# The eight new tokens' tile moved to second place in the output projection, its high and low halves in one stationary operand

## The chip, the cores and the metric

The kernel runs on one core of a Trainium2 chip. The metric is the device time of one execution in microseconds; the kernel before has a median of 1685.89 us over three runs.

## What is computed

One layer of a decoder for 1024 prompt tokens and 8 new tokens (`x_sample`), D = 1024. The part that matters comes after the two branches have been mixed:

```python
mix = jax.nn.sigmoid(ga) * y_conv + jax.nn.sigmoid(gb) * y_attn
x = x + mix @ w_o
x = x + hier_moe(rms_norm(x, norm2_g), w_rg, b_rg, w_re, b_re, w_gate, w_up, w_down)
```

`hier_moe` picks for each token one of 4 groups and two of its 8 experts (32 experts in all), and adds their weighted outputs. All products are taken in full fp32 accuracy.

## The kernel before

The 1032 tokens lie in nine tiles: tiles 0 to 7 have 128 prompt tokens each, tile 8 has the 8 new tokens. A product of two fp32 matrices is made from three products of fp32r parts, hi x hi, hi x lo and lo x hi, where lo is the rest that hi leaves.

**The stage of the change** lies between the projections before it (ending at 923.7 us of the trace) and the experts' stage (from 1070.8 us). On TensorE `step_d(n)`, n = 0 to 8, multiplies tile n of `mix` with `w_o`. The tile's `mix_hi` or `mix_lo`, 128 x up to 128, is the stationary operand, and `wo_hi` or `wo_lo`, 128 x 512, moves. For each of the 8 slices k of D there are six matmuls (lines 1019, 1021 and 1023, two output halves each), so 48 for a tile, also for the tile of 8 tokens. Between them, at k = 0, 2, 4 and 5, stand the small products for the tiles before: `rank(n - 2)` (lines 973 and 974, from the picks of tile n - 2), `turn_x2(n - 1)` (line 980, transposes), `route(n - 1)` (line 989, the router's logits) and `enter(n - 2)` (line 995, expert lists). TensorE runs its program in order, and waits where such a product isn't ready for it.

**VectorE** does for each n, in this order: `residual` (line 1827, adds the projection's PSUM to x2, two instructions), `turned` (1832, copies the transposes), `place(n - 1)`, `second_norm` (1836 and 1840, which writes the one buffer `xn` and first waits until the earlier `xn` has been written to memory), `address(n - 1)`, `mix_split(n + 2)` (1803) and `choose` (1855 to 1882, some twenty short instructions, each waiting for the last, of which line 1879 writes the `picks`). ScalarE has the squares, the other half of the copy, the root, and the high part of `mix`.

**GpSimd** writes `xn` to memory for each tile (line 620; after tile 0 also 120 filler rows, line 635), enters tokens into lists in memory by indirect DMA (626), and after the ninth tile waits for all writes of `xn` and for `gidx`, then gathers the rows of experts 0 and 1 (643). **SyncE** loads four weight chunks of 1 MB before and during step 1 (the fourth after `proj_done` 1), writes each x2 to memory (492), loads five more chunks as soon as the ninth projection is done (480), and goes on with the rest only when both gathers have landed (502 and 503). TensorE bridges the wait with `keep_busy`, then `turn_x(0)` (line 1048) needs the first gather.

Of the kernel before, what the change touches and what calls it, by code (L numbers as in the profile page):

```python
# [53 lines left out]
    0, 128, 256, 257, 265, 281, 313, 331, 347, 355, 356, 365, 365, 493)  # L54

# [51 lines left out]
def program(nc, x_prompt, x_sample, cache_conv, cache_k, cache_v, norm1_g, w_in, conv_w, w_conv_out,  # L107
# [11 lines left out]
    with ExitStack() as ctx:  # L119
# [273 lines left out]
        def _(sp):  # L393
# [152 lines left out]
        def _(pool):  # L546
# [75 lines left out]
            def enter_lists(n, rows):  # L622

                pool.wait_ge(adr_done, n + 1)
                for k in range(2):
                    pool.indirect_dma_start(out=list_dram, out_offset=bass.IndirectOffsetOnAxis(ap=adr[0:rows, 2 * n + k:2 * n + k + 1], axis=0),
                                            in_=tok_u[0:rows, 2 * n + k:2 * n + k + 1], in_offset=None,
                                            bounds_check=LISTROWS * NE - 1, oob_is_err=False).then_inc(listed, 16)

            for n in range(NT):  # L630
                if n >= 2:
                    enter_lists(n - 2, P)
                write_xn(n, P if n < 8 else B8)
# [34 lines left out]
            for n in range(NT - 2, NT):  # L668
                enter_lists(n, P if n < 8 else B8)
# [48 lines left out]
        def _(pe):  # L718
# [258 lines left out]
            def turn_x2(n, rows):  # L977
                pe.wait_ge(x2_done, n + 1)
                for k in range(KT):
                    mm = pe.transpose(bank[4 + k // 4][:, P * (k % 4):P * (k % 4) + rows], x2[0:rows, n, P * k:P * k + P], ident[0:rows, 0:rows])  # L980
# [18 lines left out]
            def step_d(n, rows):  # L999
# [1090 lines left out]
```

## Time and profile before

| | us |
|---|---|
| median of 3 runs | 1685.89 |
| lowest, highest | 1684.85, 1685.95 |
| span of the profiled execution | 1682.9 |

The span is 3.0 us under the median. It is that of the trace's first to last record; what lies outside is outside the trace.

| engine | busy us | share |
|---|---|---|
| TensorE matmul | 1613.2 | 96% |
| VectorE | 1104.4 | 66% |
| ScalarE | 845.3 | 50% |
| GpSimd | 231.8 | 14% |

The shares are means over stages with different limits. Of the chain of work that ended last 88% is TensorE and 6% DMA. The stretches and single waits below say more than the shares. In the rows, `[0.66 <-ACT rms L1360]` means that the engine sat idle for 0.66 us before this instruction, until ScalarE's line 1360 released it. A matmul's printed duration includes the overlap with its neighbours; the chain's pieces don't overlap.

### The profile page before, as it was taken

The numbers are of one execution on the slowest core, as the hardware profiler recorded it, in microseconds if no ns is written. First come the engines' busy times: TensorE is split into PE (matmuls) and PEld (weight loads), VectorE is DVE, ScalarE is ACT, GpSimd is POOL, SyncE is SP. The second block draws the span as 40 slices with busy tenths as digits, with TensorE's granted clock in tenths as the row PEclk, the third lists the DMA queues.
The fourth block names the chain that finished last, engine by engine and source line by source line (L and its number), as shares of the span: only waits on it lengthen the run. The fifth ranks groups of instructions, "written<-read, shape, count | busy, mean of one in ns | idle before, by whom it ended". The sixth has DMA issues, their size and how long they took to land.

```text
span 1682.9 us, 26202 instructions
## 1 busy us (share of the span) xinstructions
PE 1613.2 (96%) x9427; PEld 1470.9 (87%) x9427; DVE 1104.4 (66%) x1967; ACT 845.3 (50%) x1234; POOL 231.8 (14%) x245
## 2 busy tenths in 40 slices
PE   5999999999999999999999999799999999999992
PEld 4999999999999999999999887688888888877781
DVE  5332588888887232114214676898998998888893
ACT  6011366666665321112112211678878778778783
POOL 1111011110110000000000111322122122232310
PEclk9999999999999999999999999799999999999996
DMA  5252111111112111131113712999999999999966
GB/s 151 72 137 79 55 51 51 50 49 39 50 50 88 30 39 50 50 137 52 50 50 126 291 71 82 357 393 379 370 377 376 380 375 379 369 373 370 361 222 224
DMA packets 131857, 305.30 MB, mean 181 GB/s; under 512 B 30404, under 2 KB 92080, under 8 KB 106936
## 3 DMA queue, kind: packets, MB, share of 16 engines
q1 hardware_dynamic: 115415, 267.76, 43.3%
q0 software_dynamic: 16384, 36.76, 7.5%
q8 instruction: 37, 0.61, 0.2%
q14 instruction: 21, 0.16, 0.0%
HBM read 282.81 MB, written 40.41 MB: 192 GB/s over the span
## 4 chain that ended last, share of the span: by engine, by line
PE 88%; DMA 6%; DVE 3%; issue 1%; ACT 1%; SPq 0%; DVEq 0%; POOLq 0%; ACTq 0%
PE bank L725 10%; PE bank L727 9%; PE bank L726 9%; PE bank L1071 8%; PE bank L1059 6%; PE bank L1061 6%; PE bank L1060 6%; PE bank L871 5%; PE bank L873 5%; PE bank L872 5%; DMA e_raw<-in_w_e_gate_dram 5%; PE bank L1019 2%; PE bank L1021 2%; PE bank L1023 2%; PE bank L832 2%; PE bank L1048 1%
## 5 line engine op out<-in xcount | busy, mean ns | idle before, releaser
L1967 DVE TENSOR_TENSOR e_lo<-e_raw,e_hi 128x2048 fp32r<-128x2048 f32 x192 | 433.4, 2288 | 55.4 <-ACT e_hi L1378 52.5
L1378 ACT ACTIVATE e_hi<-e_raw 128x2048 fp32r<-128x2048 f32 x192 | 364.5, 1920 | 50.0 <-DMA e_raw<-in_w_e_gate_dram 20.0
L1167 ACT ACTIVATE w_hi<-w_raw 128x1024 fp32r<-128x1024 f32 x68 | 71.6, 1054 | 325.5 <-DMA w_raw<-in_w_in_dram 182.2
L1493 DVE TENSOR_TENSOR w_lo<-w_raw,w_hi 128x1024 fp32r<-128x1024 f32 x68 | 83.2, 1223 | 203.4 <-ACT w_hi L1167 203.4
L1059 PE MATMUL bank<-e_hi,xT_hi 128*128 128x512 f32 x512 | 205.4, 401 | 3.4 <-DVE xT_lo L1978 3.4
L725 PE MATMUL bank<-h_hi,w_hi 128*128 128x344 f32 x624 | 202.5, 324 | 1.1 <-DVE h_lo L1512 1.1
L1061 PE MATMUL bank<-e_hi,xT_lo 128*128 128x512 f32 x512 | 201.5, 394 | 0.0
L1060 PE MATMUL bank<-e_lo,xT_hi 128*128 128x512 f32 x512 | 201.3, 393 | 0.0
L726 PE MATMUL bank<-h_lo,w_hi 128*128 128x344 f32 x624 | 199.6, 320 | 0.0
L727 PE MATMUL bank<-h_hi,w_lo 128*128 128x344 f32 x624 | 199.6, 320 | 0.0
L871 PE MATMUL bank<-h_hi,w_hi 128*128 128x344 f32 x576 | 190.2, 330 | 0.0
L873 PE MATMUL bank<-h_hi,w_lo 128*128 128x344 f32 x576 | 184.2, 320 | 0.0
L872 PE MATMUL bank<-h_lo,w_hi 128*128 128x344 f32 x576 | 184.1, 320 | 0.0
L725 PEld LDWEIGHTS bank<-h_hi,w_hi 128*128 128x128 f32 x624 | 117.8, 189 | 5.0 <-issue 3.5
L1059 PEld LDWEIGHTS bank<-e_hi,xT_hi 128*128 128x128 f32 x512 | 96.2, 188 | 26.6 <-issue 6.2
L727 PEld LDWEIGHTS bank<-h_hi,w_lo 128*128 128x128 f32 x624 | 117.8, 189 | 0.0
L726 PEld LDWEIGHTS bank<-h_lo,w_hi 128*128 128x128 f32 x624 | 117.6, 188 | 0.0
L1061 PEld LDWEIGHTS bank<-e_hi,xT_lo 128*128 128x128 f32 x512 | 96.1, 188 | 22.9
L1060 PEld LDWEIGHTS bank<-e_lo,xT_hi 128*128 128x128 f32 x512 | 96.2, 188 | 20.6
L872 PEld LDWEIGHTS bank<-h_lo,w_hi 128*128 128x128 f32 x576 | 108.7, 189 | 0.0
L871 PEld LDWEIGHTS bank<-h_hi,w_hi 128*128 128x128 f32 x576 | 108.5, 188 | 0.0
L873 PEld LDWEIGHTS bank<-h_hi,w_lo 128*128 128x128 f32 x576 | 108.2, 188 | 0.0
(351 smaller groups left out, 3164.3 us busy)
## 6 DMA issues: line engine op xcount, KB each, us to landing
e_raw<-in_w_e_gate_dram SPq DMA_DIRECT2D x64, 1024.0 KB, 19.9
e_raw<-in_w_e_up_dram SPq DMA_DIRECT2D x64, 1024.0 KB, 21.1
e_raw<-in_w_e_down_dram SPq DMA_DIRECT2D x64, 1024.0 KB, 21.6
w_raw<-in_w_in_dram SPq DMA_DIRECT2D x104, 256.0 KB, 3.3
a_spill<-y_sb POOLq DMA_DIRECT2D x8, 516.0 KB, 4.0
a_raw<-a_spill SPq DMA_DIRECT2D x2, 2064.0 KB, 12.9
x_tok<-in_x_prompt_dram SPq DMA_DIRECT2D x4, 1024.0 KB, 10.7
w_raw<-in_w_attn_out_dram SPq DMA_DIRECT2D x32, 128.0 KB, 3.0
```

The lines of the kernel that those rows point to most:

```text
L725: pe.matmul(out, wh, xh, start=i == 0, stop=False)
L726: pe.matmul(out, wh, xl, start=False, stop=False)
L727: mm = pe.matmul(out, wl, xh, start=False, stop=i == len(pairs) - 1)
L871: pe.matmul(DN[c][:, 0:CH], w_hi[:, (s + 1) % 3, k, :], h_hi[:, k, cols], start=k == 0, stop=False)
L872: pe.matmul(DN[c][:, 0:CH], w_hi[:, (s + 1) % 3, k, :], h_lo[:, k, cols], start=False, stop=False)
L873: mm = pe.matmul(DN[c][:, 0:CH], w_lo[:, (s + 1) % 3, k, :], h_hi[:, k, cols], start=False, stop=k == KT - 1)
L1059: pe.matmul(out, xT_hi[:, par, kk, :], wh, start=kk == 0, stop=False)
L1060: pe.matmul(out, xT_hi[:, par, kk, :], wl, start=False, stop=False)
L1061: mm = pe.matmul(out, xT_lo[:, par, kk, :], wh, start=False, stop=kk == KT - 1)
L1071: mm = pe.matmul(bank[first_bank + x][:, :], a[:, kk, :], w[:, 1024 * k + 512 * x:1024 * k + 512 * x + 512], start=st, stop=kk == 3 and a ...
L1378: A.activation(e_hi[:, slot % 4, :], e_raw[slot][:, :], ACT.Copy).then_inc(e_hi_done, 1)
L1967: V.tensor_tensor(e_lo[slot][:, :], e_raw[slot][:, :], e_hi[:, slot % 4, :].bitcast(F32), ALU.subtract).then_inc(e_lo_done, 1)
```

## The change

The order of the tiles becomes 0, 8, 1, 2, ... 7 (`TILE`). What was indexed by n is indexed by `TILE[n]`, and `ROWS_AT[n]` gives a tile's tokens. For the tile of 8 tokens the high part lies in columns 0 to 7 and the low part in columns 32 to 39 of one stationary operand of 40 columns (columns 8 to 31 are set to zero). One pass over `wo_hi` and one over `wo_lo` give both parts' products, in 32 matmuls; the rows 0 to 7 and 32 to 39 of PSUM are both added to x2 by VectorE, in four instructions for two. The ninth tile is now tile 7, with 128 tokens. The filler rows of the sums come from tile 0.

```diff
+TILE = (0, 8, 1, 2, 3, 4, 5, 6, 7)
+ROWS_AT = tuple(8 if t == 8 else 128 for t in TILE)
...
-            def begin_sums(n, rows):
+            def begin_sums(n):
+                rows, tile = ROWS_AT[n], TILE[n]
                 sp.wait_ge(x2_done, n + 1)
-                sp.dma_start(sum_rows[0:rows, n, :], x2[0:rows, n, :]).then_inc(sums_begun, 16)
+                sp.dma_start(sum_rows[0:rows, tile, :], x2[0:rows, tile, :]).then_inc(sums_begun, 16)
 
             for n in range(8):
-                begin_sums(n, P)
-            sp.dma_start(sum_rows[B8:P, 8, :], x2[B8:P, 7, :]).then_inc(sums_begun, 16)
+                begin_sums(n)
+            sp.dma_start(sum_rows[B8:P, 8, :], x2[B8:P, 0, :]).then_inc(sums_begun, 16)
...
-                    begin_sums(8, B8)
+                    begin_sums(8)
                     for par in range(2):
                         sp.wait_ge(gathered[par], 16)
...
-            def write_xn(n, rows):
+            def write_xn(n):
+                rows, tile = ROWS_AT[n], TILE[n]
                 pool.wait_ge(xn_done, n + 1)
-                pool.dma_start(xn_rows[0:rows, n, :], xn[0:rows, :]).then_inc(xn_written, 16)
...
@@ -1004,17 +1011,22 @@
...
                     if k == 0 and n >= 2:
-                        rank(n - 2, par, P)
+                        rank(n - 2, par, ROWS_AT[n - 2])
                     if k == 2 and n >= 1:
-                        turn_x2(n - 1, P)
+                        turn_x2(n - 1, ROWS_AT[n - 1])
                     if k == 4 and n >= 1:
                         if n == 1:
                             pe.wait_ge(router_loaded, 96)
-                        route(n - 1, P)
+                        route(n - 1, ROWS_AT[n - 1])
...
                     if k == 5 and n >= 2:
-                        enter(n - 2, par, P)
+                        enter(n - 2, par, ROWS_AT[n - 2])
+                    half = [slice(0, 512), slice(512, D)]
+                    if TILE[n] == 8:
+                        for w, last in ((wo_hi, False), (wo_lo, k == KT - 1)):
+                            for x in range(2):
+                                mm = pe.matmul(bank[2 * par + x][0:40, :], mh[:, k, 0:40], w[:, k, half[x]], start=k == 0 and not w is wo_lo, stop=last)
+                        continue
                     out = [bank[2 * par + x][0:rows, :] for x in range(2)]
-                    half = [slice(0, 512), slice(512, D)]
                     for x in range(2):
                         pe.matmul(out[x], mh[:, k, 0:rows], wo_hi[:, k, half[x]], start=k == 0, stop=False)
                     for x in range(2):
...
-                step_d(n, P if n < 8 else B8)
+                step_d(n, ROWS_AT[n])
             rank(7, 1, P)
-            turn_x2(8, B8)
-            route(8, B8)
+            turn_x2(8, P)
+            route(8, P)
             enter(7, 1, P)
-            rank(8, 0, B8)
-            enter(8, 0, B8)
+            rank(8, 0, P)
+            enter(8, 0, P)
...
-                    A.activation(mix_hi[:, n % 2, :, 0:rows], mix[:, :, n * P:n * P + rows], ACT.Copy).then_inc(mix_hi_done, 1)
+                    at0 = TILE[n] * P
+                    A.activation(mix_hi[:, n % 2, :, 0:rows], mix[:, :, at0:at0 + rows], ACT.Copy).then_inc(mix_hi_done, 1)
...
-            mix_split(1, P)
+            mix_split(1, B8)
             for n in range(NT):
-                rows = P if n < 8 else B8
+                rows = ROWS_AT[n]
...
@@ -1800,7 +1813,11 @@
             def mix_split(n, rows):
                 dve.wait_ge(mix_hi_done, n + 1)
                 hi, lo = (mix_hi[:, n % 2, :, 0:rows], mix_lo[:, n % 2, :, 0:rows]) if n else (mix0_hi[:, :, :], mix0_lo[:, :, :])
-                V.tensor_tensor(lo, mix[:, :, n * P:n * P + rows], hi.bitcast(F32), ALU.subtract).then_inc(mix_lo_done, 1)
+                if TILE[n] == 8:
+                    V.memset(mix_hi[:, n % 2, :, B8:32].bitcast(F32), 0.0)
+                    lo = mix_hi[:, n % 2, :, 32:32 + B8]
+                at0 = TILE[n] * P
+                V.tensor_tensor(lo, mix[:, :, at0:at0 + rows], hi.bitcast(F32), ALU.subtract).then_inc(mix_lo_done, 1)
...
             def residual(n, rows):
                 dve.wait_ge(proj_done, n + 1)
-                dve.wait_ge(x_loaded[n // 2], 32)
+                dve.wait_ge(x_loaded[TILE[n] // 2], 32)
+                if TILE[n] == 8:
+                    for x in range(2):
+                        dst = x2[0:rows, 8, 512 * x:512 * x + 512]
+                        ins = V.tensor_tensor(dst, dst, bank[2 * (n % 2) + x][32:32 + rows, :], ALU.add)
+                    step.after(ins)
                 for x in range(2):
-                    dst = x2[0:rows, n, 512 * x:512 * x + 512]
+                    dst = x2[0:rows, TILE[n], 512 * x:512 * x + 512]
                     ins = V.tensor_tensor(dst, dst, bank[2 * (n % 2) + x][0:rows, :], ALU.add)
                 ins.then_inc(x2_done, 1)
...
-            mix_split(1, P)
+                V.tensor_copy(adr[0:r, 2 * TILE[n]:2 * TILE[n] + 2], adr_f[0:r, :]).then_inc(adr_done, 1)
+
+            mix_split(1, B8)
...
-                rows = P if n < 8 else B8
+                rows = ROWS_AT[n]
...
                 if n > 0:
-                    address(n - 1, (n - 1) % 2, P)
+                    address(n - 1, (n - 1) % 2, ROWS_AT[n - 1])
                 if n + 2 < NT:
-                    mix_split(n + 2, P if n + 2 < 8 else B8)
+                    mix_split(n + 2, ROWS_AT[n + 2])
                 choose(n, n % 2, rows)
-            place(8, 0, B8)
...
-            address(8, 0, B8)
+            address(8, 0, P)
```

**TensorE, step 1.** The first rows below are before, from the last of step 0 over step 1's slices k = 0 and 1 and the transposes of tile 0 (line 980) to its slice k = 2; `x_131` is x2, `bank` is PSUM.

```order
L1023 MATMUL bank<-wo_hi,mix_lo 128x512 x2
L1019 MATMUL bank<-wo_hi,mix_hi 128x512 x2
L1021 MATMUL bank<-wo_lo,mix_hi 128x512 x2
L1023 MATMUL bank<-wo_hi,mix_lo 128x512 x2
L980 MATMUL bank<-tab,x_131 128x128 x8
L1019 MATMUL bank<-wo_hi,mix_hi 128x512 x2
L1021 MATMUL bank<-wo_lo,mix_hi 128x512 x2
L1023 MATMUL bank<-wo_hi,mix_lo 128x512 x2
L1019 MATMUL bank<-wo_hi,mix_hi 128x512 x2
```

After, where lines 1027 and 987 are the new tile's matmuls and the transposes:

```order
L1035 MATMUL bank<-wo_hi,mix_lo 128x512 x2
L1027 MATMUL bank<-wo_hi,mix_hi 40x512 x2
L1027 MATMUL bank<-wo_lo,mix_hi 40x512 x2
L1027 MATMUL bank<-wo_hi,mix_hi 40x512 x2
L1027 MATMUL bank<-wo_lo,mix_hi 40x512 x2
L987 MATMUL bank<-tab,x_131 128x128 x8
L1027 MATMUL bank<-wo_hi,mix_hi 40x512 x2
L1027 MATMUL bank<-wo_lo,mix_hi 40x512 x2
```

The transposes of tile 0 now stand behind eight matmuls of step 1 instead of twelve; so do, further on, the router's products, and step 1 ends sixteen matmuls sooner.

**VectorE, behind `choose` of tile 0.** Before:

```order
L1879 TENSOR_TENSOR picks<-hots 128x32 [waits dve_step]
L1882 TENSOR_SCALAR hv<-hots,tab 128x32 x4
L1827 TENSOR_TENSOR x_131<-x_131,bank 128x512 [waits x_loaded0,proj_done]
L1827 TENSOR_TENSOR x_131<-x_131,bank 128x512
L1832 COPY h2T<-bank 128x512 [waits xnT_psum]
```

After (the adds of step 1 are lines 1845 and 1849):

```order
L1901 TENSOR_TENSOR picks<-hots 128x32 [waits dve_step]
L1904 TENSOR_SCALAR hv<-hots,tab 128x32 x4
L1845 TENSOR_TENSOR x_131<-x_131,bank 8x512 [waits x_loaded4,proj_done]
L1845 TENSOR_TENSOR x_131<-x_131,bank 8x512
L1849 TENSOR_TENSOR x_131<-x_131,bank 8x512 [waits dve_step]
L1849 TENSOR_TENSOR x_131<-x_131,bank 8x512
L1854 COPY h2T<-bank 128x4x8 [waits xnT_psum]
```

The step has two adds more, and the second pair waits for the first.

**GpSimd, the last writes and the first gathers.** Before:

```order
L626 DMA token_lists<-tok_u,adr 36864x1 [waits adr_done]
L626 DMA token_lists<-tok_u,adr 36864x1
L620 DMA normed_rows<-xn 8x1024 [waits xn_done]
L643 DMA xg<-normed_rows,gidx 128x1024 [waits gidx_done,sq2_done,xn_written]
L643 DMA xg<-normed_rows,gidx 128x1024
L626 DMA token_lists<-tok_u,adr 36864x1 [waits adr_done]
```

After (lines 626, 650 and 633 are the write, the gather and the lists):

```order
L633 DMA token_lists<-tok_u,adr 36864x1 [waits adr_done]
L633 DMA token_lists<-tok_u,adr 36864x1
L626 DMA normed_rows<-xn 128x1024 [waits xn_done]
L650 DMA xg<-normed_rows,gidx 128x1024 [waits gidx_done,sq2_done,xn_written]
L650 DMA xg<-normed_rows,gidx 128x1024
L633 DMA token_lists<-tok_u,adr 36864x1 [waits adr_done]
```

The last write of `xn`, on which both gathers wait, has 128 rows where it had 8.

## Rows read from the trace of the kernel before

**Rows 1.** Stretches: us, busy us of PE, PEld, DVE, ACT, POOL, PEclk, DMA, GB/s.
```profile
943.50:955.50 12.00, 12.00 (x61) 10.05 (x61) 7.43 (x40) 2.88 (x5) 1.07 (x2) 1.00 1.01 404
1050.00:1064.00 14.00, 5.12 (x45) 3.96 (x43) 10.93 (x65) 6.69 (x9) 1.36 (x2) 0.61 0.91 363
1064.00:1070.00 6.00, 4.84 (x23) 4.72 (x24) 4.23 (x14) 0.60 (x1) 4.78 (x5) 0.50 0.49 163
1450.00:1500.00 50.00, 49.15 (x230) 39.73 (x229) 43.82 (x29) 38.20 (x33) 15.19 (x8) 1.00 1.01 374
```

**Rows 2.** Chain that ended last, steps 1 to 3: start us, us, what.
```profile
941.46 1.71 PE bank L989 x16
...
944.18 0.46 PE bank L1023 x2
...
948.74 0.14 PE bank L973 x2
...
963.26 0.14 PE bank L973 x2
```

**Rows 3.** Timeline, tile 0 beside step 1: start us, us, engine, line, operation.
```profile
939.29 0.46 DVE L1911 TENSOR_TENSOR wr<-wr,cols 128x288 f32<-128x288 f32 x1 [2.85 <-DMA slot_no<-in_table_dram]
...
941.00 0.16 DVE L1836 RECIPROCAL rms<-rms 128x1 f32<-128x1 f32 x1 [0.66 <-ACT rms L1360]
...
947.64 0.19 DVE L1879 TENSOR_TENSOR picks<-hots 128x32 f32<-128x32 f32 x1
...
948.77 1.28 DVE L1827 TENSOR_TENSOR x<-x,bank 128x512 f32<-128x512 f32 x2 [0.34 <-PE bank L1023]
```

**Rows 4.** Timeline, tile 1 on VectorE.
```profile
955.54 2.01 DVE L1840 SCALAR_TENSOR_TENSOR xn<-x,rms,g2b 128x1024 f32<-128x1024 f32 x1 [1.42 <-DMA normed_rows<-xn]
...
962.43 0.19 DVE L1879 TENSOR_TENSOR picks<-hots 128x32 f32<-128x32 f32 x1
```

**Rows 5.** Landing of line 635's DMA: filler rows of xn, issued at 944.07.
```profile
DMA to landing us min/median/max: 11.4/11.4/11.4
```

**Rows 6.** Landing of line 620's DMA: tile 0's xn, issued at 943.53.
```profile
DMA to landing us min/median/max: 8.9/8.9/8.9
```

**Rows 7.** Timeline, tile 7's copy, then the tail with the new tokens' tile.
```profile
1039.48 0.69 DVE L1832 COPY h2T<-bank 128x512 f32<-128x512 f32 x1 [2.26 <-PE bank L980]
...
1050.19 1.27 DVE L1827 TENSOR_TENSOR x<-x,bank 8x512 f32<-8x512 f32 x2 [1.48 <-PE bank L1023]
...
1051.97 0.19 DVE L1832 COPY h2T<-bank 128x32 f32<-128x32 f32 x1 [0.51 <-PE bank L980]
...
1052.22 0.99 PE L989 MATMUL bank<-wr,h2T 128*8 128x36 f32 x16
...
1053.22 2.01 DVE L1840 SCALAR_TENSOR_TENSOR xn<-x,rms,g2b 8x1024 f32<-8x1024 f32 x1
...
1055.53 0.59 POOL L620 DMA_DIRECT2D normed_rows<-xn  x1 [8.79 <-DVE xn L1840]
...
1062.12 0.19 DVE L1926 SCALAR_TENSOR_TENSOR gidx<-slots,lst_g 128x32 uint32<-128x32 f32 x1
...
1063.22 1.08 POOL L643 DMA_INDIRECT xg<-normed_rows,gidx  x1 [7.11 <-DVE gidx L1926]
...
1068.08 1.91 PE L1048 MATMUL bank<-tab,xg 128*128 128x128 f32 x8
...
1069.78 0.34 SPq L480 DMA_DIRECT2D e_raw<-in_w_e_down_dram  x1
```

**Rows 8.** Landing of line 620's DMA: the new tokens' xn, issued at 1055.53.
```profile
DMA to landing us min/median/max: 5.5/5.5/5.5
```

**Rows 9.** Landing of line 643's first gather, issued at 1063.22.
```profile
DMA to landing us min/median/max: 4.4/4.4/4.4
```

**Rows 10.** Chain that ended last, in the experts' stage.
```profile
1462.66 27.35 DMA e_raw<-in_w_e_gate_dram
```

More of the change, by code:

```diff
@@ L616, in _, with enter_lists @@
             pool.memset(idle_in[:, :], 0.0).then_inc(idle_ready, 1)
-            def write_xn(n, rows):
+            def write_xn(n):
+                rows, tile = ROWS_AT[n], TILE[n]
                 pool.wait_ge(xn_done, n + 1)
-                pool.dma_start(xn_rows[0:rows, n, :], xn[0:rows, :]).then_inc(xn_written, 16)
-            def enter_lists(n, rows):
+                pool.dma_start(xn_rows[0:rows, tile, :], xn[0:rows, :]).then_inc(xn_written, 16)
+            def enter_lists(n):
+                rows, tile = ROWS_AT[n], TILE[n]
                 pool.wait_ge(adr_done, n + 1)
                 for k in range(2):
-                    pool.indirect_dma_start(out=list_dram, out_offset=bass.IndirectOffsetOnAxis(ap=adr[0:rows, 2 * n + k:2 * n + k + 1], axis=0),
-                                            in_=tok_u[0:rows, 2 * n + k:2 * n + k + 1], in_offset=None,
+                    pool.indirect_dma_start(out=list_dram, out_offset=bass.IndirectOffsetOnAxis(ap=adr[0:rows, 2 * tile + k:2 * tile + k + 1], axis=0),
+                                            in_=tok_u[0:rows, 2 * tile + k:2 * tile + k + 1], in_offset=None,
                                             bounds_check=LISTROWS * NE - 1, oob_is_err=False).then_inc(listed, 16)
@@ L631, in _ @@
                 if n >= 2:
-                    enter_lists(n - 2, P)
-                write_xn(n, P if n < 8 else B8)
+                    enter_lists(n - 2)
+                write_xn(n)
                 if n == 0:
@@ L668, in _ @@
             for n in range(NT - 2, NT):
-                enter_lists(n, P if n < 8 else B8)
+                enter_lists(n)
             pool.wait_ge(wts_done, 1)
@@ L979, in turn_x2 @@
                 for k in range(KT):
-                    mm = pe.transpose(bank[4 + k // 4][:, P * (k % 4):P * (k % 4) + rows], x2[0:rows, n, P * k:P * k + P], ident[0:rows, 0:rows])
+                    mm = pe.transpose(bank[4 + k // 4][:, P * (k % 4):P * (k % 4) + rows], x2[0:rows, TILE[n], P * k:P * k + P], ident[0:rows, 0:rows])
                     if k % 4 == 3:
@@ L1345, in mix_split @@
                 else:
-                    A.activation(mix_hi[:, n % 2, :, 0:rows], mix[:, :, n * P:n * P + rows], ACT.Copy).then_inc(mix_hi_done, 1)
+                    at0 = TILE[n] * P
+                    A.activation(mix_hi[:, n % 2, :, 0:rows], mix[:, :, at0:at0 + rows], ACT.Copy).then_inc(mix_hi_done, 1)
             def square(n, rows):
                 act.wait_ge(x2_done, n + 1)
-                A.activation(squares[0:rows, :], x2[0:rows, n, :], ACT.Square, accum_out=ssq[0:rows, 0:1]).then_inc(sq2_done, 1)
+                A.activation(squares[0:rows, :], x2[0:rows, TILE[n], :], ACT.Square, accum_out=ssq[0:rows, 0:1]).then_inc(sq2_done, 1)
             def turned(n, rows):
@@ L1838, in second_norm @@
                     dve.wait_ge(xn_written, n * 16 + 16)
-                src = x2[0:rows, n, :].rearrange("t (p k) -> t p k", k=KT)
+                src = x2[0:rows, TILE[n], :].rearrange("t (p k) -> t p k", k=KT)
                 V.scalar_tensor_tensor(xn[0:rows, :].rearrange("t (k p) -> t p k", p=P), src, rms[0:rows, 1:2],
@@ L1869, in choose @@
                 step.after(V.max(top_e[0:r, :], e8[0:r, :]))
-                V.tensor_copy(tv[0:r, :, n:n + 1], top_e[0:r, 0:2].unsqueeze(2))
+                V.tensor_copy(tv[0:r, :, TILE[n]:TILE[n] + 1], top_e[0:r, 0:2].unsqueeze(2))
                 step.after(V.max_index(idx_e[0:r, :], top_e[0:r, :], e8[0:r, :]))
@@ L1880, in choose @@
                 for k in range(2):
-                    for a, col in enumerate((C_TOK + 2 * n + k, C_ROW + n)):
+                    for a, col in enumerate((C_TOK + 2 * TILE[n] + k, C_ROW + TILE[n])):
                         V.tensor_scalar(hv[0:r, par, k, a, :], hots[0:r, par, k, :], tab[0:r, col:col + 1], None, ALU.mult)
@@ L1913, in _ @@
                 if n > 0:
-                    place(n - 1, (n - 1) % 2, P)
+                    place(n - 1, (n - 1) % 2, ROWS_AT[n - 1])
                 second_norm(n, rows)
                 if n > 0:
-                    address(n - 1, (n - 1) % 2, P)
+                    address(n - 1, (n - 1) % 2, ROWS_AT[n - 1])
                 if n + 2 < NT:
-                    mix_split(n + 2, P if n + 2 < 8 else B8)
+                    mix_split(n + 2, ROWS_AT[n + 2])
                 choose(n, n % 2, rows)
-            place(8, 0, B8)
+            place(8, 0, P)
             def slots_of(dst, src, blank):
```

3 lines of the change are left out of this document (1 added, 2 removed).

## The prediction

> **What bounds the kernel now.** I read the stretches first, then the chain of waits, then the timeline around the two ends of the projection stage, and last the landings of the DMAs that something there waits for. In steps 1 to 8 of the projection TensorE is the bound: the stretch 943.5 to 955.5 has it busy for all 12.00 us at the full clock, and the chain lies on it from step 1 to step 3 [rows 1, 2]. Two things there are close behind it. VectorE's picks of tile 0 are ready at 947.83 (947.64 + 0.19) and TensorE's rank product, which needs them, starts at 948.74; those of tile 1 are ready at 962.62, and the rank product starts at 963.26 [rows 2 to 4]. So VectorE is only 0.9 and 0.64 us ahead. And VectorE itself was held at tile 1 for 1.42 us by a DMA: it could write `xn` only at 955.54, when tile 0's 128 rows and the 120 filler rows had reached memory (944.07 + 11.4 = 955.5), while 404 GB/s of weights and rows filled the DMA engines [rows 1, 4, 5]. After the ninth projection comes a tail of another kind: TensorE is busy for 5.12 of 14 us, and the end is set by VectorE's chain from the last residual (1050.19) to `gidx` (done at 1062.31), the gather that starts at 1063.22 and lands at 1067.6 (+ 4.4), and the second gather, behind which SyncE goes on with the weights at 1069.78 [rows 1, 7, 9]. From there both TensorE and the DMA engines have no pause: in 1450 to 1500 the DMA share is 1.01 and TensorE loses 0.85 of 50 us, and the chain has pieces such as 27.35 us of one weight DMA [rows 1, 10]. What this stage is worth is therefore read from one thing: when the gathers land. TensorE's first expert and the weight stream both start from them.
>
> **Step 1: what is removed.** Two 512-column matmuls take 0.46 us of the chain, 0.23 each [rows 2]. Sixteen fewer are 3.7 us. The stationary operand has 40 columns where the tile had 8; the trace has no such matmul, but those of 128 columns keep the pace of 0.23, so it lies between two forms and I count nothing for it. Twelve of the sixteen stand behind the transposes. Four stand ahead of them, so the transposes of tile 0 and ScalarE's root come 0.9 us sooner.
>
> **Step 1: what is given back at once.** TensorE would reach the router's products at 941.46 less 8 x 0.23, at 939.6 [rows 2]. The half of `h2T` that VectorE copies can't be there: VectorE is held by the last small load until 939.29, scales `wr` for 0.46 us, and a copy takes 0.69 us [rows 3, 7], so it ends at 940.4. TensorE waits 0.8 us. It then ends step 1 at 948.74 - 3.7 + 0.8 = 945.8. The next instruction is the rank product on tile 0's picks. VectorE gains at most the 0.66 us that it sat idle for the root [rows 3], since the `wr` scaling stays where it is: picks at 947.2. TensorE waits another 1.4 us, and everything of step 2 is queued behind that wait. **Step 2 begins 1.5 us sooner, not 3.7.**
>
> **Step 2: the DMA in the way.** VectorE adds the new tokens' rows in four instructions of 0.64 us (1.27 for two at 8 rows [rows 7]), 2.6 us for 1.28, from 947.8 to 950.4. TensorE wants them after a rank and 12 matmuls, at about 950.4, so this costs nothing; with a later pick its cover is gone, and it would cost up to 1.3. The transposes and router products of 8 rows are shorter (0.99 for 1.71 [rows 2, 7]), 0.7 us more on TensorE's side. But VectorE must again wait for the write of tile 0's `xn` and the filler rows. It is issued at most 0.66 us sooner and shares the engines with the same weight chunks. The x2 write of this step shrinks from 512 to 32 KB, which can help the landing a little. I take 0.5 us sooner (between 0, and 1.4 where all of VectorE's idle there goes). Behind it come `xn`, a split and `choose`, as before, so the picks of tile 1 come at 962.1, 0.5 sooner. The rank product had 0.64 us of slack behind them [rows 2, 4], so **step 3 begins 1.15 us sooner**, between 0.6 and the 2.3 that TensorE's work alone would allow (1.5 + 0.7 + some tenths).
>
> **Steps 3 to 8** have the same work as before on every engine, with tile 2 in place of tile 3 and so on. VectorE had waited for TensorE in them, so the 1.15 us stays until the ninth projection ends: at 1049.0. SyncE then issues the same five chunks.
>
> **The tail: what is added.** The last tile has 128 rows. VectorE's copy takes 0.69 for 0.19 [rows 7], the second half on ScalarE grows alike, and the short instructions of `choose` some hundredths each: `xn` is done 0.55 us and `gidx` about 0.7 us later after the last residual than now. So `gidx` is done at 1062.3 - 1.15 + 0.7 = 1061.9, and the write of the last `xn` is issued at 1055.53 - 1.15 + 0.55 = 1054.9. The write of 8 rows took 5.5 us, to 1061.0, 1.3 before `gidx` [rows 7, 8], and was hidden. A write of 128 rows against a full weight stream is in the trace as well: tile 0's, 8.9 us [rows 6], against the same kind of load (363 GB/s in the tail's stretch, 404 there [rows 1]). Bounds are 5.5 (8 rows) and 11.4 (the filler rows behind tile 0's [rows 5]). I take 8.9, since rows and load are alike: it lands at 1063.8, **1.9 us after `gidx`**, and becomes what the gather waits for. Now 0.9 us lie from `gidx` to the gather's start; the gather starts at 1064.7 for 1063.2, 1.5 us later, and so do the second gather and SyncE's next loads. TensorE had 0.5 us to spare at `turn_x` (gather landed at 1067.6, transposes from 1068.08), so it starts 1.0 later. The lists of tile 7 are entered behind the gathers, with 128 rows for 8: a few tenths of DMA work that I leave in the range. The write of the last x2, 512 for 32 KB, isn't waited for by the gathers.
>
> **The sum**, against the profiled execution: -3.7 (16 matmuls) + 0.8 (h2T) + 1.4 (picks of tile 0) + 0.35 (of picks of tile 1, after the 0.7 of smaller products is spent too) = -1.15; + 0.7 (tail on VectorE) + 1.95 (the write that now lands after `gidx`) = +1.5. The span goes from 1682.9 to 1684.4. What lies outside it, 3.0 us, stays, so the median goes from 1685.89 to 1687.4.
>
> **Rivals.** (a) **The last write gets its turn.** The two writes after tile 0, 992 KB in 12.0 us, got 83 GB/s, a fifth of the 404 [rows 1, 5]. If the queue of GpSimd instead had half of the engines' time beside the weights, the 480 KB more than in the 8-row write would take 2.4 us at 202 GB/s on top of 5.5: landing at 1062.8, gather 0.5 later than now, 1686.4; if it is faster still, `gidx` decides, 0.45 sooner, 1685.4. Time: 1685.9. The Trainium skill ("DMA: Bandwidth & Descriptors", section on queues, rings and completion order) says that each DMA engine takes turns between the queues that have work, a packet from each. By that rule this rival would be the forecast; rows 5 speak against equal shares in bytes. (b) **TensorE's gain comes through.** If VectorE's picks don't hold step 2 and 3 (the landing comes 1.4 sooner and the copy isn't late) and the write is hidden, -3.7 - 0.7 + 0.7 remains: 1682.2. Against it is that the waits follow from end times that the change leaves where they are. (c) **The last write is served behind the weights.** Five chunks of 1 MB are issued first, and 512 KB of x2 go in behind them; if the write takes the 11.4 us of the filler rows, it lands at 1066.3 and the gather starts 4.0 later: 1689.9. TensorE would then idle between `keep_busy` and the first gather at the low clock (0.50 in 1064 to 1070 [rows 1]), where eight transposes took 1.91 us, which adds up to a microsecond. This is slower by more than 0.2% from a landing 10.8 us after issue.
>
> **How the numbers follow.** A measurement of this kernel can tell about 0.2%, 3.4 us, from no change. Forecast, 1686.4 to 1689: 0.45. Rival (a), about 1685.9: 0.27. Rival (b), 1682.2: 0.12, at the border of faster; I count 0.10 of it and 0.02 of the rest as faster. Rival (c), about 1690: 0.16, of which nearly all is slower; 0.02 more for the forecast's upper end. Faster 0.12, same 0.70, slower 0.18. The range runs from 1683.3 to 1690.4; outside lie most of (b) and a little beyond (c). The forecast's own range is 1686.0 to 1689.0.
>
> **What would show it.** In the changed kernel's trace: TensorE idle for 0.8 us before the router's products of step 1 and for 1.4 before the rank product of step 2; VectorE's `xn` of the second tile still released by the DMA of `normed_rows`, near 955; the ninth projection ending near 1049; the last write of `xn` landing 8 to 10 us after issue, and the first gather released by it, not by `gidx`, near 1064.7. The prediction is wrong if the write lands before `gidx` (then the time is 1685.4 or less), if TensorE has no wait in steps 1 and 2, or if the experts' stage isn't moved by what its first gather is moved by.

## The result

The median goes from 1685.59 to 1688.97 us, over eleven runs of each in turn on the same chip. The ratio is 1.0022, with a 95% interval from 1.0014 to 1.0030, so 2.4 to 5.1 us more. That lies on the bound of 0.2% that the prediction drew between no change and slower. The forecast was 1687.4, +1.5: direction and range held, but the forecast size is less than half of the 3.4 us that came.

The profiled execution has a span of 1685.7 us, for 1682.9. It was the fastest of the eleven (1687.26 us), 1.7 us under their median. One thing must be known before the rows are compared: in this profile everything ahead of the change lies 1.0 us earlier. The first residual of the stage (VectorE's adds of tile 0) starts at 935.15 in the kernel before and at 934.14 in the changed one:

```profile
935.15 1.29 DVE L1827 TENSOR_TENSOR x<-x,bank 128x512 f32<-128x512 f32 x2 [5.51 <-PE bank L1023]
```

```profile
934.14 1.29 DVE L1849 TENSOR_TENSOR x<-x,bank 128x512 f32<-128x512 f32 x2 [5.83 <-PE bank L1035]
```

Such shifts come from one execution to the next, also of the same kernel: the start lies between 934.1 and 937.4 in the profiles here, and a second profile of the changed kernel has it at 935.17. So I count from the first residual in both, and write +114.7 for 114.7 us after it. "Step n" is the projection of the n-th tile, counted from 0, with the small products between its matmuls; the ninth residual is VectorE's adds behind the last projection.

**The stretches** of the changed kernel, those that answer to [rows 1] (us; busy us of PE, PEld, DVE, ACT, POOL; PEclk, DMA share, GB/s):

```profile
942.50:954.50 12.00, 10.98 (x67) 7.60 (x66) 8.05 (x43) 2.43 (x5) 0.57 (x2) 1.00 1.00 402
1048.85:1062.85 14.00, 7.70 (x41) 6.83 (x40) 10.79 (x57) 6.81 (x7) 0.58 (x1) 0.63 0.93 362
1062.85:1068.85 6.00, 3.49 (x17) 3.00 (x18) 4.92 (x22) 0.33 (x2) 3.79 (x3) 0.50 0.84 303
1450.00:1500.00 50.00, 49.00 (x227) 39.30 (x226) 43.86 (x29) 38.54 (x33) 14.30 (x8) 1.00 1.01 369
```

TensorE, full in steps 1 and 2 before (12.00 of 12.00), has now a pause of 1 us in them. In the last 6 us before the first expert the DMA engines are busy for 0.84 of the time and not for 0.49: the last chunks and the last write are still under way in it.

**The timeline from step 1 to step 3**, which answers to [rows 3, 4]. Lines 1933, 1854 and 1862 are the scaling of `wr`, the copy to `h2T` and `xn`; 996 the router's products, 980 `rank`, 1845 and 1849 the adds.

```profile
938.51 0.46 DVE L1933 TENSOR_TENSOR wr<-wr,cols 128x288 f32<-128x288 f32 x1 [3.09 <-DMA slot_no<-in_table_dram]
939.72 1.95 PE L996 MATMUL bank<-wr,h2T 128*128 128x36 f32 x16 [1.03 <-DVE h2T L1854]
946.11 0.19 DVE L1901 TENSOR_TENSOR picks<-hots 128x32 f32<-128x32 f32 x1
946.40 0.38 PE L980 MATMUL bank<-picks,tab 128*128 128x32 f32 x2 [1.02 <-issue]
946.90 1.28 DVE L1845 TENSOR_TENSOR x<-x,bank 8x512 f32<-8x512 f32 x2
948.22 1.27 DVE L1849 TENSOR_TENSOR x<-x,bank 8x512 f32<-8x512 f32 x2
954.10 2.05 DVE L1862 SCALAR_TENSOR_TENSOR xn<-x,rms,g2b 8x1024 f32<-8x1024 f32 x1 [2.65 <-DMA normed_rows<-xn]
961.13 0.21 PE L980 MATMUL bank<-picks,tab 8*8 8x32 f32 x2 [0.97 <-issue]
```

TensorE waits three times where it waited nowhere: 1.03 us for `h2T`, 1.02 for tile 0's picks ("issue" here, but the picks end at 946.30 and the product starts at 946.40), and 0.97 for the new tokens' picks, behind an `xn` that the DMA held for 2.65 us. The chain that ended last now begins its part here on the small load for which the `wr` scaling waits (start, us, what):

```profile
929.57 8.92 DMA slot_no<-in_table_dram
...
938.51 0.46 DVE wr L1933
938.97 0.61 DVE h2T L1854
...
939.72 1.95 PE bank L996 x16
```

**The tail**, which answers to [rows 7] (line 980 is the rank product, 1911 VectorE's reading of it, 626 writes `xn`, 650 gathers, 1060 is `turn_x`, 484 on SPq the weight load behind both gathers):

```profile
1048.85 1.29 DVE L1849 TENSOR_TENSOR x<-x,bank 128x512 f32<-128x512 f32 x2 [1.66 <-PE bank L1035]
...
1051.64 3.00 PE L996 MATMUL bank<-wr,h2T 128*128 128x36 f32 x16 [0.35 <-DVE h2T L1854]
1052.65 2.05 DVE L1862 SCALAR_TENSOR_TENSOR xn<-x,rms,g2b 128x1024 f32<-128x1024 f32 x1
...
1055.00 0.58 POOL L626 DMA_DIRECT2D normed_rows<-xn  x1 [9.79 <-DVE xn L1862]
...
1058.65 0.63 PE L980 MATMUL bank<-picks,tab 128*128 128x32 f32 x2 [3.11 <-DVE picks L1901]
1059.10 0.61 PE L981 MATMUL bank<-seen,tab 128*128 128x32 f32 x2
...
1059.76 0.18 DVE L1911 CUSTOM_DVE_ANT_0 prod<-hots,bank 128x32 f32<-128x32 f32 x1 [0.57 <-issue]
...
1062.37 0.19 DVE L1948 SCALAR_TENSOR_TENSOR gidx<-slots,lst_g 128x32 uint32<-128x32 f32 x1
...
1064.45 1.07 POOL L650 DMA_INDIRECT xg<-normed_rows,gidx  x1 [8.88 <-DMA normed_rows<-xn]
...
1068.74 1.40 PE L1060 MATMUL bank<-tab,xg 128*128 128x128 f32 x8
...
1071.12 0.33 SPq L484 DMA_DIRECT2D e_raw<-in_w_e_down_dram  x1
```

And the landing of the write issued at 1055.00, which answers to [rows 6, 8]:

```profile
DMA to landing us min/median/max: 8.6/8.6/8.6
```

The gather was released by `gidx` before and is released by the write now: the write landed at 1063.6, 1.0 us after `gidx` (1062.56).

The same marks, counted from the first residual:

| mark | before | changed | moved |
|---|---|---|---|
| rank of step 2 | +13.42 | +12.26 | -1.16 |
| rank of step 3 | +27.95 | +26.99 | -0.96 |
| ninth residual starts | +115.04 | +114.71 | -0.33 |
| last write of `xn` issued | +120.38 | +120.86 | +0.48 |
| `gidx` done | +127.16 | +128.42 | +1.26 |
| first gather starts | +128.07 | +130.31 | +2.24 |
| weight stream goes on | +134.63 | +136.98 | +2.35 |
| end of the span | +747.75 | +751.56 | +3.8 |

### The profile page after: what moved, and what is told of

The parts are those of the page before. It is cut to its first block, busy times and chain, and to the rows that moved or that the text cites. A ratio compares the mean times of both kernels' runs of the same rounds, so it can differ in the third digit from the quotient of the medians.

```text
span 1685.7 us, 26173 instructions
## 1 busy us (share of the span) xinstructions
PE 1612.9 (96%) x9411; PEld 1470.2 (87%) x9411; DVE 1105.9 (66%) x1970; ACT 845.4 (50%) x1234; POOL 235.6 (14%) x245
## 4 chain that ended last, share of the span: by engine, by line
PE 82%; DMA 12%; DVE 3%; issue 1%; ACT 1%; SPq 0%; POOL 0%; DVEq 0%; POOLq 0%; ACTq 0%
PE bank L732 9%; PE bank L734 9%; PE bank L733 9%; PE bank L1083 7%; DMA e_raw<-in_w_e_gate_dram 7%; PE bank L878 5%; PE bank L880 5%; PE bank L879 5%; PE bank L1071 5%; PE bank L1073 5%; PE bank L1072 5%; PE bank L1031 2%; PE bank L839 2%; PE bank L1033 2%; PE bank L1035 2%; DMA e_raw<-in_w_e_down_dram 1%
```

## The experiments

Times are medians. Each ratio is to the kernel before, timed in turn on the same chip; gains and costs in us are taken from the ratios. The edits are to the changed kernel unless said otherwise.

### The two parts apart: order, and joint operand

**The new tokens' tile last again, in 32 matmuls.**

```diff
-TILE = (0, 8, 1, 2, 3, 4, 5, 6, 7)
+TILE = (0, 1, 2, 3, 4, 5, 6, 7, 8)
```

(with `ROWS_AT[8]` for the fixed 128 in the tail's calls)

> The side-by-side product alone: the new tokens' tile keeps its ninth place, and has 32 matmuls for 48. Theory (the end follows the moment at which both gathers have landed, and that follows VectorE's tail and the last write of xn): TensorE ends the ninth projection 3.7 us sooner, VectorE is then still busy with choose of tile 7 and starts its four adds about 3.2 us sooner, ends them 1.9 us sooner; the last write stays at 8 rows and hidden; the weight stream goes on 1.9 us sooner and the median is 1.9 us lower, ratio 0.9989. Rival (the 40-column form itself or the four adds are what cost): ratio 1.000 or above. Rival (TensorE's 3.7 us all come through): 0.9978.

Measured: 1683.67 us, ratio 0.9992 (0.9983 to 1.0001).

```profile
1047.52 1.28 DVE L1845 TENSOR_TENSOR x<-x,bank 8x512 f32<-8x512 f32 x2
1048.83 1.27 DVE L1849 TENSOR_TENSOR x<-x,bank 8x512 f32<-8x512 f32 x2
...
1054.16 0.59 POOL L626 DMA_DIRECT2D normed_rows<-xn  x1 [8.02 <-DVE xn L1862]
1061.86 1.07 POOL L650 DMA_INDIRECT xg<-normed_rows,gidx  x1 [7.11 <-DVE gidx L1948]
```

The ninth residual starts at +112.05, 2.99 us sooner than before; the four adds in a row take 1.3 of it back, `gidx` releases the gather as before, and it starts 1.68 sooner. The ratio shows 1.4 us of that, at the edge of what can be told.

**The order alone, all nine tiles in 48 matmuls.**

```diff
-                    if TILE[n] == 8:
+                    if False:
```

(the same at the adds and in `mix_split`)

> The move alone: the new tokens' tile is second, with its 48 matmuls and two adds as before. Theory: no waits of TensorE in steps 1 and 2 or shorter ones, the ninth projection ends where it did in the kernel before (within 0.5 us), the tail is the changed kernel's (write of 128 rows, lands 8.6 us after its issue, gather after it), the first gather starts 3 us later than before; median 3.5 to 4.5 us above before, ratio 1.0024, 0.5 to 1 us above the changed kernel. Rival (the loss of the changed kernel comes from waits that its shorter step brings): ratio 1.000.

Measured: 1687.96 us, ratio 1.0012 (1.0004 to 1.0021).

```profile
1065.52 1.07 POOL L650 DMA_INDIRECT xg<-normed_rows,gidx  x1 [8.55 <-DMA normed_rows<-xn]
```

The ninth residual starts at +114.99, for +114.71 in the changed kernel, and the first gather at +130.25, for +130.31. So in second place the sixteen matmuls buy 0.3 us at the ninth residual and nothing that can be seen at the gather, and the order is what costs. I had expected 0.5 to 1 us more than in the changed kernel; the median is 1.0 lower, and the two intervals overlap.

**The new tokens' tile fifth**, `TILE = (0, 1, 2, 3, 8, 4, 5, 6, 7)`: away from the load of the router's table and from the filler rows, with 128 rows last.

> The changed kernel with the new tokens' tile in fifth place instead of second (order 0, 1, 2, 3, 8, 4, 5, 6, 7), where the DMA engines are nearly idle. Theory (in the changed kernel the four matmuls' worth that step 1 gained is cut by the late small load, by VectorE's picks and by the write of tile 0's xn against the weight chunks): VectorE's xn behind the short step has no DMA wait, only the picks hold TensorE, by about 1.5 us; the ninth projection ends 2.2 to 2.9 us sooner than in the kernel before, for 0.3 us in the changed kernel. The tail is the changed kernel's, so the first gather starts at 128.1 us after the first residual (changed 130.3, before 128.1) and the weight stream goes on at 134.8 (changed 137.0); median 0 to 0.5 us above before, ratio 1.0002. Rival (the place of the tile doesn't matter, the product's form gives what it gives): ratio as the changed kernel, 1.002.

Measured: 1686.27 us, ratio 1.0008 (0.9999 to 1.0017).

```profile
1047.87 1.28 DVE L1849 TENSOR_TENSOR x<-x,bank 128x512 f32<-128x512 f32 x2 [1.67 <-PE bank L1035]
...
1063.56 1.07 POOL L650 DMA_INDIRECT xg<-normed_rows,gidx  x1 [8.96 <-DMA normed_rows<-xn]
```

The ninth residual starts at +112.05 here too, with the one wait for picks of 0.84 us. What second place kept of the 2.99 us was 0.33. The tail of 128 rows, from there to the gather, takes 15.7 us, for 13.0 before: it gives back 2.7. In all eight profiles with this tail behind a weight stream of four chunks or more it took 15.3 to 16.1. One thing here stays unexplained: the gather starts at +127.74, 0.33 us sooner than in the kernel before, and yet the ratio says 1.4 us longer (0.2 less to 2.9 more).

### What the last write costs

**The kernel before, with 128 rows in the last write** (line 620), nothing else changed.

```diff
-                pool.dma_start(xn_rows[0:rows, n, :], xn[0:rows, :]).then_inc(xn_written, 16)
+                pool.dma_start(xn_rows[:, n, :], xn[:, :]).then_inc(xn_written, 16)
```

> The kernel before, whose last write of xn takes all 128 rows of the buffer instead of 8 (the 120 more go to filler rows, nothing else differs). Theory: the write lands about 8.6 us after its issue at 1055.5, at 1064.1, 1.8 us after gidx; the first gather starts at 1065.0 for 1063.2, the weight stream goes on at 1071.6 for 1069.8, and the median is 1.8 us above before, ratio 1.0011. Rival (the order of the tokens in the lists, or the rest of the changed kernel's tail, is what costs): the write is still hidden, ratio 1.0000.

Measured: 1687.58 us, ratio 1.0008 (0.9999 to 1.0016).

```profile
1057.16 0.58 POOL L620 DMA_DIRECT2D normed_rows<-xn  x1 [8.81 <-DVE xn L1840]
1063.75 0.19 DVE L1926 SCALAR_TENSOR_TENSOR gidx<-slots,lst_g 128x32 uint32<-128x32 f32 x1
1067.12 1.06 POOL L643 DMA_INDIRECT xg<-normed_rows,gidx  x1 [9.38 <-DMA normed_rows<-xn]
```

The wide write takes 9.1 us for 5.5, and the gather starts 3.2 us behind `gidx` instead of 0.9, so 2.3 later. The ratio shows 1.4 of that, and its interval just takes in no change.

**Four weight chunks ahead of the gate instead of five** (`if s == 8`):

> The changed kernel with four chunks of weights issued ahead of the gate for five, so that one MB less stands before the last write of xn. Theory: the write lands 1 to 2 us sooner after its issue (8.6 to about 7), the gather starts up to 1.1 us sooner, then released by gidx; but a chunk (1 MB, 2.5 us of the DMA engines at about 400 GB/s) moves behind the gap, and since the experts' stage ends by the weight stream the median is 1.4 us above the changed kernel. Rival (only the time of the first gather counts): 1 us below the changed kernel. Rival (the write isn't held by the chunks): it lands 8.6 us after its issue as before.

Measured: 1691.19 us, ratio 1.0033 (1.0022 to 1.0044). The write took 9.1 us again: four chunks cover 10 us from the ninth projection's end, and the write is issued 6 us after it. This one couldn't tell whether the stream makes the write slow; two chunks could.

**The x2 write behind the gate** (`begin_sums(8)` after the waits for the gathers):

> The changed kernel with the last write of x2 (512 KB) behind the gate instead of ahead of it. If this write, issued 3 us ahead of the last write of xn, is what holds that one: it lands 1 to 2 us sooner than 8.6 us after its issue, and the first gather starts about 1 us sooner; but the 512 KB now stand ahead of the next chunk, 1.3 us, so the median stays within 0.5 us of the changed kernel. Rival (the write is slow by its own size or its own queue): 8.6 us as before, and the median 1 us above the changed kernel.

Measured: 1688.71 us, ratio 1.0023 (1.0011 to 1.0035). The landing is 8.7 us, so the 512 KB of x2 ahead of it are not what slows it.

**Two chunks ahead of the gate** (`if s == 6`), so that the stream has run dry:

> The changed kernel, but SyncE issues two weight chunks instead of five between the ninth projection and its wait for the gathers (the x2 write behind them as before), so the weight stream has run out by about the time that the last xn write is issued (2 MB at 404 GB/s are 5 us, the write comes 6 us after the projection's end). If contention with the stream makes the write slow (theory), it lands 3 to 5 us after issue instead of 8.3 to 9.1, gidx decides the gather, and the first gather starts 29.2 to 29.6 us after step 3 of the chain used here, that is 0.9 to 1.0 after gidx as in the kernel before; the weight stream, three chunks poorer, costs 5 to 8 us later, so the time is 1693 to 1698. If the 8.6 us are the write's own price whatever else runs (rival), it lands at 8 or more again and the gather stays released by it.

Measured: 1693.31 us, ratio 1.0050 (1.0034 to 1.0065). Landing and gather, then the stretch of the write (columns PE, PEld, DVE, ACT, POOL, PEclk, DMA, GB/s):

```profile
DMA to landing us min/median/max: 5.8/5.8/5.8
```

```profile
1066.05 1.07 POOL L650 DMA_INDIRECT xg<-normed_rows,gidx  x1 [7.91 <-DVE gidx L1948]
...
1057.56:1063.36 5.80, 1.10 (x5) 0.97 (x5) 4.71 (x36) 1.99 (x2) 0.58 (x1) 0.66 0.67 256
```

With the DMA engines at 0.67 for 1.02 (the changed kernel, 1055.0 to 1063.6, 411 GB/s) the write lands 2.8 us sooner and `gidx` decides again, 0.9 us ahead of the gather. So the stream is what makes the write late. The 3 to 5 us that I expected were too few; the DMA engines were still busy for two thirds of the time. The kernel before has a write of 128 rows beside even less traffic: the one issued at 957.84, in step 2, landed in 2.9 us with the DMA engines at 0.45, its own rows included. The run with two chunks also shows what a late stream costs: its first gather starts 1.0 us sooner than in the changed kernel and TensorE's first `turn_x` 0.3 us sooner (+134.30 for +134.60), but with three chunks behind the gate for ahead of it the time is 4.7 us longer than the changed kernel's (8.4 for 3.7 us above the kernel before).

### Where the loss is carried to the end

**Only the first 8 of the last tile's 128 tokens entered behind the gathers.** The ninth tile is prompt tile 7 here; its other 120 tokens' entries of the lists are left out.

```diff
-                enter_lists(n)
+                enter_lists(n, B8 if n == 8 else None)
```

> The changed kernel with only 8 of the last tile's 128 tokens entered into the lists in memory (two indirect DMAs; the lists serve only experts with over 128 tokens). It leaves out 120 tokens' entries. If these entries, at 1070 us in the weight stream, are what makes the stretch from the stream's going on to the end 614.6 us for 613.1 before: the stretch is 613 to 613.5 and the median 1 to 1.5 us below the changed kernel. Rival (that stretch differs from run to run by as much): unchanged median within 0.5 us, stretch anywhere between 613 and 615.

Measured: 1689.05 us, ratio 1.0019 (1.0010 to 1.0029), for 1.0022 in the changed kernel. No gain that can be told. The stretch from the weight stream's restart to the end is 613.4 us in its profile, as expected for a gain, but the changed kernel without this edit has had 612.5 as well (the last run below), so the larger lists are not shown to cost anything.

**Six chunks ahead of the gate**, in three kernels. With the new tokens' tile last, 32 matmuls:

```diff
-                if s == 9:
+                if s == 10:
```

> e1_last with six chunks of weights ahead of the gate instead of five, one MB more for the gap in which the DMA engines are half idle. Theory by the gap (DMA share 0.49 from 1064 to 1070): the sixth chunk is done while the gathers are issued, they land up to 1.5 us later, and the stream behind the gap is one MB, 2.5 us, shorter: median 1 us below e1_last, 1.0 to 3 below before, ratio 0.9986. Rival (the gathers are held by all of the chunk's 2.5 us, and TensorE's start with them): no gain over e1_last or a loss.

Measured: 1682.78 us, ratio 0.9987 (0.9978 to 0.9996). The same line in the kernel before:

> The kernel before, with six weight chunks instead of five ahead of the gate. If the six chunks alone gave the gain of the run with the new tokens' tile last and six chunks (0.9987, e6_last_six), this gives the same: 1682.5 to 1683.5. If the 32 matmuls for 48 at the ninth tile have a part in it, this stays 1.0 to 2.5 above, at 1684 to 1685.5. If a sixth chunk is worth nothing here, 1685.3 to 1686.

Measured: 1686.52 us, ratio 1.0013 (1.0004 to 1.0022). And in the changed kernel:

> The changed kernel with six chunks ahead of the gate. The last xn write now has a full stream for all of its way (until about 1066): landing 8.5 to 9.5 after issue, gather as late as in the changed kernel or up to 0.8 later. If the loss of the change is the stream's late restart, the sixth chunk (2.6 us of stream) covers most of it: 1685.5 to 1687 for 1689. If the loss sits on TensorE's side (its first expert begins 1.7 later and stays so), the sixth chunk gives at most 1: 1688 to 1689.

Measured: 1689.46 us, ratio 1.0024 (1.0014 to 1.0033).

The first gather of each, by its landing (tile last, before, changed; 4.4 and 4.2 us with five chunks):

```profile
DMA to landing us min/median/max: 4.9/4.9/4.9
```

```profile
DMA to landing us min/median/max: 6.9/6.9/6.9
```

```profile
DMA to landing us min/median/max: 6.3/6.3/6.3
```

And what TensorE does with it in the kernel before and in the changed one, both with six chunks:

```profile
1069.10 1.97 PE L1048 MATMUL bank<-tab,xg 128*128 128x128 f32 x8 [1.86 <-DMA xg<-normed_rows,gidx]
```

```profile
1073.46 1.97 PE L1060 MATMUL bank<-tab,xg 128*128 128x128 f32 x8 [2.12 <-DMA xg<-normed_rows,gidx]
```

A sixth chunk is no gift: where the chunks are issued at +115 they are still under way when the gather is, it lands 2 us later, and TensorE waits at the low clock (granted clock 0.50, in the kernel before from 1062 to 1069, in the changed one from 1067.0 to 1073.4). With the tile last in 32 matmuls they are issued at +111.6, 3.5 us sooner, and the gather meets only their end. In the kernel before the sixth chunk cost 2.2 us (0.7 to 3.7). In the changed kernel neither cost nor gain can be told (1.0024 for 1.0022), though TensorE's first `turn_x` starts 1.9 us later. With the tile last it cost nothing: 2.2 us gained (0.7 to 3.7), for 1.4 with five chunks (0.2 lost to 2.9 gained), so whether it helped there isn't shown. This version, the new tokens' tile last, 32 matmuls and six chunks, is the only one here whose interval lies below the kernel before, by 0.04 to 0.22%.

**The changed kernel profiled again:**

> The changed kernel once more, for a second profile: which numbers repeat. If the waits of TensorE before the router's products (1.03), before the rank of step 2 (1.02) and of step 3 (0.97) and the write's 8.6 us belong to the kernel, they come within 0.2 and 0.6. The stretch from the weight stream's restart to the end (614.6; 613.1 in the kernel before) may come out between 613 and 615; if it is 614.3 or more again, the second 1.5 us of the loss lie in the experts' stage, if it is near 613.1 they are scatter between executions.

Measured: a span of 1685.5 us, and 1687.09 in its one timed run, for a median of 1684.77 of the kernel before.

```profile
940.46 0.46 DVE L1933 TENSOR_TENSOR wr<-wr,cols 128x288 f32<-128x288 f32 x1 [4.01 <-DMA slot_no<-in_table_dram]
941.67 1.95 PE L996 MATMUL bank<-wr,h2T 128*128 128x36 f32 x16 [1.96 <-DVE h2T L1854]
948.34 0.38 PE L980 MATMUL bank<-picks,tab 128*128 128x32 f32 x2 [1.02 <-issue]
...
1051.02 1.28 DVE L1849 TENSOR_TENSOR x<-x,bank 128x512 f32<-128x512 f32 x2 [1.67 <-PE bank L1035]
...
1066.59 1.07 POOL L650 DMA_INDIRECT xg<-normed_rows,gidx  x1 [8.84 <-DMA normed_rows<-xn]
```

The first residual starts at 935.17 here, as in the kernel before, so these rows can be laid beside [rows 7] as they are. Two things don't repeat. The small load lands 0.9 us later after the first residual, TensorE waits 1.96 us for `h2T`, and the ninth residual starts at 1051.02, 0.83 *later* than before, with sixteen matmuls fewer. And from the weight stream's restart (1073.0) to the end it is 612.5 us, for 614.6 in the first profile and 613.1 in the kernel before.

## Why the prediction was right, and where it was short

**TensorE's gain in step 1 is mostly given back: right.** Expected were a wait of 0.8 for `h2T`, 1.4 for tile 0's picks and a step 3 that begins 1.15 sooner. Measured: 1.03, 1.02 and 0.96. The mechanism is shown from the other side by the run with the tile in fifth place, which keeps 2.99 us. The wait for `h2T` is no fixed number, though: it goes with a small load's landing, and was 0.33, 0.96, 1.03, 1.03, 1.29, 1.96 and 0.26 in the seven profiles with this order and 32 matmuls. Where it is short, the picks wait longer (1.38 to 1.42), so step 2 began 0.9 to 1.5 us sooner in six of the seven, and 0.25 in the seventh.

**"Steps 3 to 8 have the same work as before on every engine": this step failed.** The lead fell from 0.96 to 0.33 us. 0.27 of it is the last of them: rank to rank was 14.26 us in the kernel before (100.58 to 114.84 after the first residual) for 14.53 in the steps of 128 rows, since its tile had 8. The changed kernel has a tile of 128 there, 14.52. I had taken the work to be the same in the last step too. The other 0.36 went in step 3 (14.89 us), in which TensorE handles the new tokens' rank and lists. Almost all of it, 0.34, lies around the list products (line 1002): from the matmuls ahead of them to the first pair behind them it is 2.72 us (969.64 to 972.36), for 2.38 in a step with 128 tokens there (971.60 to 973.98 in the kernel before). The products of 8 tokens are the longer ones (the changed kernel, then the one before):

```profile
971.20 0.65 PE L1002 MATMUL bank<-hv,onehot_s 8*128 8x64 f32 x4
```

```profile
973.07 0.55 PE L995 MATMUL bank<-hv,onehot_s 128*128 128x64 f32 x4
```

Why they take longer is open. The step that holds the new tokens' rank and lists took 14.86 us in the run with the order alone and 14.88 with the tile fifth, so this comes with the place of the tile and not with the joint operand.

**The tail on VectorE was put at +0.7 and is +1.6: mis-sized.** From the ninth residual to `gidx` it is 13.71 us for 12.12 (both from the residual's start). 0.81 of it come before the write is issued, for the 0.55 forecast: beside the copy, TensorE's transposes take 1.10 us for 0.66. 0.18 are VectorE's short instructions, as forecast. The other 0.60 had been put at nothing: VectorE waits 0.57 us for the rank products (the row at 1059.76), where it was still busy before. They run at the low clock in both kernels (granted clock 0.50), and take 0.63 and 0.61 us, where the kernel before has

```profile
1059.02 0.27 PE L973 MATMUL bank<-picks,tab 8*8 8x32 f32 x2 [4.78 <-DVE picks L1879]
1059.22 0.28 PE L974 MATMUL bank<-seen,tab 128*8 128x32 f32 x2
```

The router's products take 3.00 us for 0.99 [rows 7], but they end at 1054.64, while VectorE is still busy with `xn` and the addresses, and don't hold the chain.

**The last write takes the place of `gidx`: right**, with 8.6 us for the 8.9 taken from tile 0's write. It was 8.3 to 9.1 in all kernels with 128 rows last and a running stream. Because `gidx` is later than I thought, the write lands only 1.0 us after it, not 1.9. Rival (c), 11.4 us, falls with it. Rival (a) has the same release and a landing of 7.9 us; the landings lie 0.4 to 1.2 us above that, so only its size is off. The Trainium skill ("DMA: Bandwidth & Descriptors", "Queues, rings and completion order") has each DMA engine take turns between queues, packet by packet. Rival (a) had 5.5 us for the first 8 rows and 2.4 for the other 480 KB, at half of 404 GB/s: 7.9. Measured were 3.1 to 3.6 us for these 480 KB (8.6 and 9.1 less 5.5), 137 to 159 GB/s, a third or a little more of 411. That lies between the half of rival (a) and the fifth that I took from [rows 5]; most of the landing is the 5.5 us that even 8 rows take beside the stream. The order of packets the trace doesn't show. Rival (b) falls with the three waits.

**The sum at the gather**: -0.33 (lead) + 1.59 (tail) + 0.98 (write) = +2.24, for the forecast's +1.5. The error is the lead and the tail, 0.8 and 0.9 us, less 1.0: the later `gidx` runs beside the write and hides that much of its landing. The two profiles of the changed kernel, and those with the late x2 write and the short lists, which have the same five chunks, have the gather at +130.2 to +131.4, so +2.1 to +3.35, 2.5 in the mean.

**"Read from one thing: when the gathers land" is too narrow.** It holds only for the same chunks ahead of the gate: with two of them the gather came 1.0 us sooner than in the changed kernel and the time was 4.7 us longer.

**What lies outside the span isn't 3.0 us.** In every timed run on record with a span beside it the time is 1.5 to 1.7 us more than the span. By that the profiled execution of the kernel before was itself some 1.4 us faster than its median (an estimate). The forecast adds the same 3.0 to both sides, so its +1.5 isn't touched.

**From the gather to the end: what stays open.** The stream's restart moved as the gather did (+2.35). TensorE is 1.3 us later from the second `turn_x` (+145.47 for +144.14) up to 1450 us (+501.38 for +500.07). Only then, where the chain lies on weight DMAs [rows 10], the distance grows, to 1.6 and 2.0 at the next two, then to between 2.2 and 3.5, with 3.1 at the last. In the second profile of the changed kernel it is 2.3 up to 1455 us, then between 2.4 and 3.5, with 2.8 at the last. That a late stream is paid is shown by the run with two chunks; that it is what the changed kernel pays is argued from the chain. The sixth chunk in the changed kernel was to cover it and gave nothing, but it also made the gather land 2 us later, so it doesn't decide. The size at the end is not settled to better than a microsecond: +3.8 in the first profile, +2.6 in the second, 3.4 (2.4 to 5.1) in the medians. A mean of 2.5 at the gather lies inside that interval; the part of 0.9 between the two figures may be scatter of the experts' stage, which took 612.5 to 614.6 us in executions of the same kernel.

## What to carry to other kernels

When work is taken from one engine in a pipeline that is balanced to a microsecond, look for a place where the others are ahead: the same sixteen matmuls were worth 0.3 us in step 1, where a small load, VectorE's picks and a DMA stood close behind, and 3.0 in the last place. What comes last in a stage has its whole latency exposed: put the smallest tile there, and count its every instruction on every engine (and at the clock that holds there), its writes included. And before more prefetch is put ahead of a gate, ask what it runs into: the same sixth chunk cost 2.2 us in one kernel and nothing in another where the chunks were issued 3.5 us sooner.

## What the runs showed of the hardware

A write of 128 rows, 512 KB, on GpSimd's queue took 8.3 to 9.1 us beside a weight stream at some 400 GB/s, 5.8 when most of the stream was gone (DMA share 0.67), and 2.9 in the quiet of step 2 (0.45); one of 8 rows took 5.5 to 5.8 beside the full stream and 2.1 in the quiet of step 2 (0.11). Whether four or five chunks were issued ahead of it made no difference (9.1 and 8.6), nor did a 512 KB write on SyncE's queue behind the gate instead of ahead of it (8.7). The first gather took 4.2 to 4.9 us where the stream was out or nearly so, and 6.3 to 6.9 beside it. A small load's landing moved by 2 us against TensorE's program between executions (the scaling that waits for it began 3.2 to 5.3 us after the first residual), and took TensorE's start with it wherever no cover was left. Two matmul passes with a stationary operand of 40 columns kept the pace of 0.23 us each of those with 128 (0.47 a pair), so on TensorE the joint operand itself is free; VectorE's two more adds are not (1.3 us in the last place).
